# One program for the close of the first layer and the attention of the second: projections of the unscaled row, latent columns first, the output product in two halves by head kind

## The reference

```python
# end of the first block
x = x + g2 * moe_ffn(h, *moe_w).reshape(x.shape)
return rms_norm(x, final_norm_g)                  # x * rsqrt(mean(x*x) + 1e-6) * g

# second block
h = _rmsnorm(x, norm_mix_pre[l])
proj = h @ w_in[l]                                # 2208 columns
qa, ka, va, c_q, c_kv, k_r = jnp.split(proj, SPLIT_POINTS, axis=-1)   # 512, 512, 512, 384, 256, 32
ya = _dilated_attention(qa, ka, va)               # 8 heads of 64, distance bias and mask
yb = _mla(c_q, c_kv, k_r, q_lat_norm[l], w_uq[l], kv_lat_norm[l], w_ukv[l])
#    q = rmsnorm(c_q) @ w_uq, kv = rmsnorm(c_kv) @ w_ukv, 32 of 96 columns of q and k turned by the
#    token's angle, softmax(q k / sqrt(96)) v, 8 heads
y = jnp.concatenate([_rmsnorm(ya, out_norm_a[l]), _rmsnorm(yb, out_norm_b[l])], axis=-1)
y = y @ w_o[l]
x = x + _rmsnorm(y, norm_mix_post[l])
h = _rmsnorm(x, norm_ffn_pre[l])
u = _dwconv(h @ w_up[l], conv_w[l], conv_b[l])    # 5632 columns, three taps over the tokens
g, v = u[..., :D_FF], u[..., D_FF:]
y = (jax.nn.gelu(g, approximate=True) * v) @ w_down[l]
x = x + _rmsnorm(y, norm_ffn_post[l])
```

## Time and profile before

| | us |
|---|---|
| median of three runs (2211.8 to 2215.29) | 2213.43 |
| the profiled execution | 2209.3 |
| its span | 2207.5 |
| TensorE busy (88% of the span) | 1943.3 |
| VectorE busy | 622.6 |
| ScalarE busy | 435.8 |

### The profile page before, as it was taken

How to read it: one execution, slowest core, us unless ns; L and a number is a source line. 1 busy time by engine, 2 the same in 40 slices (tenths; PEclk the granted TensorE clock), 3 DMA queues, 4 the chain that set the end, 5 groups by cost and what they waited for, 6 DMA issues and landing times. The chain is left out here.

```text
span 2207.5 us, 24892 instructions
## 1 busy us (share of the span) xinstructions
PE 1943.3 (88%) x9274; PEld 1051.9 (48%) x9276; DVE 622.6 (28%) x1366; ACT 435.8 (20%) x849; POOL 67.1 (3%) x86
## 2 busy tenths in 40 slices
PE   5999796998989789989899999888889597879997
PEld 2446354987878443332333333333332245557774
DVE  2376355337420311111011111111111304333223
ACT  2221641345221111101111111111101114310111
POOL 1000400100000000000000000000000000000000
PEclk9999897899999899999999999999999899889998
DMA  9443336133454579999999999999999514033442
GB/s 343 152 172 116 143 99 153 66 104 114 163 184 165 228 298 416 418 418 419 418 419 417 418 418 417 417 417 418 417 419 418 204 58 165 0 116 143 155 158 86
DMA packets 150651, 566.73 MB, mean 257 GB/s; under 512 B 35872, under 2 KB 43808, under 8 KB 112736
## 3 DMA queue, kind: packets, MB, share of 16 engines
q1 hardware_dynamic: 150592, 565.91, 66.1%
HBM read 555.26 MB, written 10.62 MB: 256 GB/s over the span
## 5 line engine op out<-in xcount | busy, mean ns | idle before, releaser
L2005 PE MATMUL expert_gb<-expert_ring,hT 128*64 128x512 f32 x1024 | 270.4, 607 | 69.5 <-DMA expert_ring<-in_w_gu 68.1
L2005 PE MATMUL expert_lb<-expert_ring,hT 128*64 128x512 f32 x1024 | 262.8, 592 | 0.0
L1910 DVE TENSOR_SCALAR hT<-expert_gb 128x512 f32<-128x512 f32 x32 | 22.1, 692 | 717.1 <-PE expert_lb L2005 717.1
L2053 PE MATMUL expert_yb<-expert_ring,hT 128*64 128x512 f32 x512 | 222.7, 592 | 1.5 <-DMA expert_ring<-in_w_down 1.4
L2053 PE MATMUL expert_yb<-expert_ring,h2T 128*64 128x512 f32 x512 | 222.8, 592 | 0.0
L2005 PEld LDWEIGHTS expert_gb<-expert_ring,hT 128*64 128x64 f32 x1024 | 59.3, 135 | 250.2 <-DMA expert_ring<-in_w_gu 200.4
L2642 PE MATMUL ffn_pu<-ffn_hT,ffn_wu 128*128 128x256 f32 x704 | 156.5, 381 | 0.0
L2642 PEld LDWEIGHTS ffn_pu<-ffn_hT,ffn_wu 128*128 128x128 f32 x704 | 134.7, 191 | 27.4 <-issue 9.6
L445 PE MATMUL mix_in_pj<-hT,mix_in_pj_ring 128*128 128x512 f32 (+1 forms) x384 | 144.0, 533 | 4.0 <-DVE hT L566 4.0
L2005 PEld LDWEIGHTS expert_lb<-expert_ring,hT 128*64 128x64 f32 x1024 | 72.8, 137 | 147.0 <-issue 147.0
L2053 PEld LDWEIGHTS expert_yb<-expert_ring,hT 128*64 128x64 f32 x512 | 69.9, 137 | 143.2 <-issue 140.4
(11 more groups left out here) (474 smaller groups left out, 2314.1 us busy)
## 6 DMA issues: line engine op xcount, KB each, us to landing
expert_ring<-in_w_gu SPq DMA_DIRECT2D x256, 1024.0 KB, 19.7
expert_ring<-in_w_down SPq DMA_DIRECT2D x128, 1024.0 KB, 20.7
fill_w<-in_w_fill SPq DMA_DIRECT2D x48, 512.0 KB, 3.7
mix_in_wm<-in_w_mod SPq DMA_DIRECT2D x11, 2048.0 KB, 9.5
ffn_wu<-in_w_up_units SPq DMA_DIRECT2D x22, 1024.0 KB, 6.2
mix_in_pj_ring<-in_w_in_units SPq DMA_DIRECT2D x12, 1024.0 KB, 4.8
ffn_wd<-in_w_down SPq DMA_DIRECT2D x22, 512.0 KB, 3.4
attend_in_wi<-in_w_in SPq DMA_DIRECT2D x4, 2048.0 KB, 10.5
```

The source lines that it names most:

```text
L1910: v.tensor_scalar(glu, gb[j][:], LIMIT, None, ALU.min).then_inc(s_glu, 1)
L2005: m = pe.matmul(b[halves[h], :], xT[:, k, x], ring[:, z, c0 + 512 * h:c0 + 512 * h + 512], start=False, stop=(k == KT - 1))
L2053: m = pe.matmul(yb[h][halves[j], :], hidT[j][:, c, hh * SLOTS:(hh + 1) * SLOTS], ring[:, z, a * F + 512 * h:a * F + 512 * h + 512], start= ...
```

## The change

Blocks 1 to 4 become one block, `attend_stage`, of which the buffers lie in tensors of the first layer (the experts' ring holds w_in's blocks, `proj`, the bias, `qz`, `ka`, and later w_o, `qb`, `kb`). In it:

- TensorE transposes `S.x` as soon as a half of it is added. The product of the final gain and the second layer's first gain (`gg`) is multiplied in by the copies to `hT`, four column groups on ScalarE (`low`) and four on VectorE (`high`). The two roots are multiplied together (`rr`) and go into the copies of the products.
- w_in's blocks are taken in the order latent columns, rest of them, q, k, v; the latent columns are transposed unscaled, and their roots multiply the expansions in VectorE's copies. The expansions stand between the last groups of projections.
- the squares of the output of the first kind of heads, its transposes and its copies stand within the softmax steps (at 10, 12, 14 and 15); the output product is split into eight groups of four, first kind first, and `join` adds the two parts with their roots. The last row work is done by halves.
- in the feed-forward stage the first two units' up products are done by halves of tokens (`ups_half`), the root per half, and the matmuls that clear the sums come first.

```diff
-def close_first_stage(nc, A, C, S):
...
-                    link(v.tensor_tensor(S.acc[:, t, :], S.acc[:, t, :], S.g2, ALU.mult))
...
+    BLOCKS = [(3 * WA, 512), (3 * WA + 512, IN2 - 3 * WA - 512), (0, 512), (WA, 512), (2 * WA, 512)]
+    X = S.g
...
+        ring = Cut(S.ring[:].rearrange("p a n -> p (a n)"))
+        wi = ring(3, KT, 512)
+        proj = ring(2, IN2)
...
+                sp.dma_start(gcol[:], A.gains2_col).then_inc(s_gc, 16)
+                block_in(0)
+                sp.dma_start(gf, A.final_norm_g.to_broadcast([P, D])).then_inc(s_gf, 16)
+                block_in(1)
+                block_in(2)
+                sp.dma_start(wuq[:], A.w_uq.rearrange("(k p) n -> p k n", p=P)).then_inc(s_up, 16)
+                sp.dma_start(wukv, A.w_ukv.rearrange("(k p) n -> p k n", p=P)).then_inc(s_up, 16)
+                sp.dma_start(rope[:], A.rope).then_inc(s_up, 16)
+                sp.wait_ge(s_p, 2)
+                block_in(3)
+                sp.dma_start(bias, A.key_bias).then_inc(s_bias, 16)
+                sp.wait_ge(s_p, 4)
+                block_in(4)
+                sp.wait_ge(s_z, 2)
+                sp.dma_start(gpost, A.norm_mix_post.to_broadcast([P, D])).then_inc(s_wo, 16)
+                sp.wait_ge(s_p, 10)
+                sp.dma_start(wo, A.w_o.rearrange("(k p) n -> p k n", p=P)).then_inc(s_wo, 16)
+
...
+                    if v == 0:
+                        pe.wait_ge(s_ha, t + 1)
+                        pe.wait_ge(s_hd, t + 1)
+                    if g >= 4:
+                        pe.wait_ge(s_c, g - 3)
+                    for k in range(KT):
+                        m = pe.matmul(flat(4 + g % 4)[:, 0:n], hT[:, k, t * P:(t + 1) * P], wi[:, v % 3, k, 0:n],
+                                      start=(k == 0), stop=(k == KT - 1))
+                    m.then_inc(s_p, 1)
...
+                for t in range(2):
+                    pe.wait_ge(s_z, t + 1)
+                    for h in range(2):
+                        for k in range(4):
+                            m = pe.transpose(bank[2 * t + h][:, k, :], S.x[:, t, (4 * h + k) * P:(4 * h + k + 1) * P], C.ident)
+                        m.then_inc(s_t, 1)
+                for v in range(3):
                     for t in range(2):
...
+                        project(v, t)
+                pe.wait_ge(s_c, 4)
...
+                for t in range(2):
+                    project(3, t)
+                expand(0)
+                project(4, 0)
+                expand(1)
+                project(4, 1)
...
+                    if n in (10, 14):
+                        turn_out(0, n // 14, pY[n // 14])
+                pe.wait_ge(s_wo, 32)
+                multiply(0, 0, 0, bank[0])
+                multiply(0, 0, 1, bank[1])
+                turn_out(1, 0, pT[0])
+                turn_out(1, 1, pT[1])
+                multiply(0, 1, 0, bank[6])
+                multiply(0, 1, 1, bank[7])
+                multiply(1, 0, 0, bank[4])
+                multiply(1, 0, 1, bank[5])
+                pe.wait_ge(s_tc, 4)
+                multiply(1, 1, 0, bank[2])
+                multiply(1, 1, 1, bank[3])
+
...
+                def low(t):
+                    act.wait_ge(s_t, 2 * t + 1)
+                    for k in range(4):
+                        m = act.activation(hT[:, k, t * P:(t + 1) * P], bank[2 * t][:, k, :], ACT.Copy, scale=gg[:, k:k + 1])
+                    m.then_inc(s_ha, 1)
...
+                def copy(v, t):
+                    c, n = BLOCKS[v]
+                    g = 2 * v + t
+                    act.wait_ge(s_p, g + 1)
+                    act.activation(proj[:, t, c:c + n], flat(4 + g % 4)[:, 0:n], ACT.Copy,
+                                   scale=rr[:, t:t + 1]).then_inc(s_c, 1)
...
+                def square_out(a, t):
+                    act.wait_ge(s_y, 2 * a + t + 1)
+                    act.wait_ge(s_ys, 2 * a + t + 1)
+                    act.activation(junk[:, 0:WA], y[:, t, a, :], ACT.Square,
+                                   accum_out=stat[:, 6 + 2 * t + a:7 + 2 * t + a]).then_inc(s_ys, 1)
...
+                act.wait_ge(s_yr, 2)
+                act.activation(rstd[:, 6:10], stat[:, 6:10], ACT.Sqrt).then_inc(s_or, 1)
+                act.wait_ge(s_or, 1)
+                for t in range(2):
+                    for h in range(2):
+                        act.wait_ge(s_po, 2 * t + h + 1)
+                        act.activation(part[:, t, h, :], flat((0, 6)[t] + h), ACT.Copy,
+                                       scale=rstd[:, 6 + 2 * t:7 + 2 * t]).then_inc(s_f, 1)
+                for t in range(2):
+                    act.wait_ge(s_yo, 2 * t + 2)
+                    act.wait_ge(s_ys, 5 + t)
+                    act.activation(junk[:], yo[:, t, :], ACT.Square, accum_out=stat[:, 10 + t:11 + t]).then_inc(s_ys, 1)
+                    act.wait_ge(s_on, 2 * t + 2)
+                    act.activation(rstd[:, 10 + t:11 + t], stat[:, 10 + t:11 + t], ACT.Sqrt).then_inc(s_or, 1)
...
+                    v.tensor_tensor(S.acc[:, t, :], S.acc[:, t, :], S.g2, ALU.mult).then_inc(s_m, 1)
+                    v.wait_ge(s_m, t + 1)
+                    v.tensor_tensor(S.x[:, t, :], S.x[:, t, :], S.acc[:, t, :], ALU.add).then_inc(s_z, 1)
+                    if t == 0:
+                        v.wait_ge(s_gc, 16)
+                        v.tensor_tensor(gg[:], gcol[:, 0:KT], gcol[:, 2 * KT + 5:], ALU.mult).then_inc(s_gg, 1)
+                v.wait_ge(s_gg, 1)
+                high(0)
...
+                    v.scalar_tensor_tensor(X[:, t, :], S.x[:, t, :], rstd[:, t:t + 1], gf, ALU.mult, ALU.mult).then_inc(s_xd, 1)
+                v.wait_ge(s_sq, 4)
+                norm(v.tensor_scalar(stat[:, 10:12], stat[:, 10:12], 1.0 / D, EPS, ALU.mult, ALU.add))
+                norm(v.reciprocal(stat[:, 10:12], stat[:, 10:12]))
+                v.wait_ge(s_rt, 2)
+                v.tensor_tensor(rr[:], rstd[:, 0:2], rstd[:, 10:12], ALU.mult).then_inc(s_rr, 1)
...
+                        m = v.tensor_scalar(qc[:, t, 4 * g:4 * g + 4, :], src, rstd[:, 2 + t:3 + t], None, ALU.mult)
...
+                    if n in (7, 11, 15):
+                        take(n // 4 - 1)
+                    if n in (12, 15):
+                        gain(0, n // 15, pY[n // 15])
...
+                def join(t):
+                    for h in range(2):
+                        v.wait_ge(s_f, 2 * t + h + 1)
+                        v.wait_ge(s_po, 4 + 2 * t + h + 1)
+                        v.scalar_tensor_tensor(yo[:, t, 512 * h:512 * h + 512], flat((4, 2)[t] + h),
+                                               rstd[:, 7 + 2 * t:8 + 2 * t], part[:, t, h, :], ALU.mult, ALU.add).then_inc(s_yo, 1)
+                    v.wait_ge(s_ys, 6 + t)
+                    last(v.tensor_scalar(stat[:, 10 + t:11 + t], stat[:, 10 + t:11 + t], 1.0 / D, EPS, ALU.mult, ALU.add))
+                    last(v.reciprocal(stat[:, 10 + t:11 + t], stat[:, 10 + t:11 + t]))
+
+                def finish(t):
+                    v.wait_ge(s_or, 2 + t)
...
+                ups_half(0, 0)
+                turn(1)
+                ups_half(1, 0)
+                for z in range(2):
+                    ups_half(z, 1).then_inc(up[z], 1)
                 with pe.Fori(0, FT // 2 - 1) as i:
-                    ups(1, i * 16 + 16)
-                    downs(0, i + 1)
-                    ups(0, i * 16 + 32)
```

824 lines of the change are left out of this document (387 added, 437 removed).

## The result

The changed kernel takes 2173.49 us (median of 4 runs, 2170.69 to 2174.06), the kernel before 2212.61 us beside it (4 runs, 2210.33 to 2215.29). The ratio is 0.9822, 95% interval 0.9809 to 0.9835: 39.1 us less. Forecast were 42.0 us less and 2171.4 us. The profiled execution took 2173.72 us, its span is 2171.1.

A forecast was written before the change was run, and what follows sets the result against it. It took a chain of waits among TensorE, VectorE and ScalarE as the bound. Terms -13.1 - 14.3 + 0.9 - 13.4 - 2.1 + 0 gave -42.0 us; from 2213.4 that is 2171.4 us, range 2163 to 2183, chance 0.60.

The forecast's parts named there:

- front: First scaling to first projection: starts at 8.5 us instead of 21.6, waiting for the first weight block; -13.1 us.
- to the scores: First projection to first scores: 85.3 us instead of 99.65, from removed waits, program ends and half clock; -14.3 us.
- softmax loop: Sixteen softmax steps: inserted transposes cost TensorE time, squares and copies fit in other engines' slack; +0.9 us, bounds 0 and 5.1.
- product: Last value matmul to output product's end: starts without a pause, 28.7 us instead of 42.1; -13.4 us.
- tail: Output product's end to last add: half the rows finished earlier, 5.6 us left of 7.7; -2.1 us.
- border of the stages: Between the attention stage's last add and the feed-forward stage; the prediction's sum has no separate term for it.
- feed-forward head: First up products, split by token halves: earlier start and costs of halving cancel; 0 us, bounds -2.5 and +2.0.
- The new wait: Ahead of k's transposes, before the scores: TensorE stands 2.8 us until ScalarE has copied qz and ka.
- The first: Rival: loop inserts cost 5.1 us, product starts at half clock (1.7), new wait drops the clock (2.0); 2179.3 us, chance 0.22.
- The second: Rival: no half clock at start (1.0), wait hidden (2.8), loop free (0.9), feed-forward head -2.5; 2164.2 us, chance 0.12.
- The third: Rival: roots come late, so projections stand waiting for copies; each us is a us back, 15 lost gives 2186; chance 0.03.
- The fourth: Rival: chip grants only half clock through projections and product, +44.7 us net, 2258 us; chance 0.03.

The follow-up runs named there:

- roots_first: Changed kernel with the first projection also waiting for the joined scale (both roots); median 2178.2 us, ratio 0.985.
- expand_last: Changed kernel with both expansions of the latents behind the last projection again, latent columns still first; median 2174.0 us, ratio 0.9832.
- front_warm: Changed kernel with products of the unit matrix with itself filling TensorE's idle time in the front; median 2169.3 us, ratio 0.9815.
- before_again: The kernel before, unchanged, profiled a second time; 239.98 us from first scaling to first down product, against 239.78 in its first trace.
- product_waits: Changed kernel with the output product waiting for the output roots and the second kind's transposes ahead of it; median 2177.6 us, ratio 0.9851.
- gpost_late_whole: Changed kernel with the earlier feed-forward head (rows in one piece) and its wide gain row asked for behind the loop; median 2170.5 us, ratio 0.9818.
- joined_warm: Changed kernel with shared copies, first block in two transfers, whole feed-forward head, late wide row and unit-matrix products in the front; median 2163.7 us, ratio 0.9784.

## Why the prediction was right

The sum was 42.0, measured are 40.1 in the stretch and 39.1 in the median. By its own steps, against the first trace of the kernel before (the second would have moved product and feed-forward head by 1.6 and 0.8 us, in opposite directions):

| step | forecast | measured | |
|---|---|---|---|
| front | -13.1 | -13.3 | first projection 8.28 us in (8.5) |
| to the scores | -14.3 | -13.5 | projections 61.8, not 60.2 |
| softmax loop | +0.9 | +0.7 | |
| product | -13.4 | -13.7 | no idle, clock 1.00 |
| tail | -2.1 | -2.4 | last add 5.3 us after the product |
| border of the stages | 0 | +0.3 | 1.16 us before, 1.50 after |
| feed-forward head | 0 | +1.6 | inside its bounds, -2.5 to +2.0 |

**Front: right, and half of the reason shown.** The block landed 7.9 us after its issue (forecast 8.0), the scale was ready 14.3 us in (14.5), and roots_first gives back 6.2 us when the product waits for it. The reason for the other 7 us rests on the chain in the trace before, which is no longer there.

**To the scores: right but for the start.** The new wait is 2.80 us for 2.8 forecast, and expand_last shows the cover on VectorE. Wrong was "projections 59.2 + 1.0 for the cold start": TensorE was busy 61.8 us with them. front_warm, at full clock through all of them, has 60.0, so 0.8 us was missing from the 59.2 and the cold start cost 1.8, not 1.0. I had read from the earlier trace rows that transposes alone leave the clock at 1.00. In the new front transposes of the same kind stand in two groups of 8 with gaps, and the clock is 0.50 at 1748.5. TensorE: Matmul & The Clock Gate, Part 4, in the Trainium skill, has it that transposes don't bring the full clock. By that rule this term would be 2.0, closer than mine. The traces are divided on the rule: behind the same 16 transposes without a gap the clock was 1.00 once and 0.50 once (before_again). So my reading rested on one of two outcomes, and whether the gaps or the kind of instruction decide, no run here shows.

**Softmax and product: right.** The product is the largest single gain. product_waits shows that a part of it hangs on the start without a pause: waits of 2.5 us in all were followed by a clock near one half, 4.6 us together. The rest of the 13.7 (transposes and copies moved into the softmax steps) is read from the row of 12.9 us that is gone; no run puts it back. The three runs that bring a wait back return 6.2, 4.0 and 4.6 us, 14.8 of the 40. The table load stands at 1879.47, under the product, for 1.28 us. Of the drain that ScalarE: Activation LUTs, What ACT_TABLE_LOAD costs, in the Trainium skill, adds to a switch, product_waits shows none: there the load begins 0.01 us behind the square's sum and the root starts 0.34 us behind the load, waiting for VectorE.

**Feed-forward head: the step that failed.** It said that the earlier start and the costs of halving cancel. The first up product starts 9.1 us behind the stage's begin where before it was 10.4, a gain of 1.3 us and not the 2 that I had: `ffn_hT` was ready for 2.2, and the weights came 0.9 us later still. I had taken the gain row for the bound and not the weights behind it in the same queue. Against the 1.3 stand four costs, 2.9 us together. The 0.9 us of transposes and VectorE's 0.44 at the end were in the forecast. Two were not. The start is at half clock for longer: it costs 2.0 us (5.63 us until the second transposes, 3.6 at 113 ns a pass) where it cost 1.2 before (14.97 us for the 64 passes against 13.81 at full clock in gpost_late_whole), 0.8 more. And 128 half passes take 14.5 us at full clock where 64 whole ones take 13.8, 0.7 more; "no gain and little loss" was too kind. An earlier landing alone would not have mended it: in front_warm the up products start 1.1 us sooner than in the changed kernel, and the first down product only 0.6.

**Rivals.** The first was right in kind, in one of its three parts: the clock did fall at the new wait in 3 of 8 traces, for 1.5 to 2.6 us where I had 2.0, though not in the changed kernel's own. The second didn't happen, though joined_warm has the first of its four parts, the warm start, and about half of two more: a wait of 1.7 us instead of 2.8, and a head 1.3 us shorter than before instead of 2.5. The third didn't: the scale came with 3.0 us to spare for its first use by ScalarE, at 1757.54. The fourth didn't: behind the start the clock is 1.00 through the projections (1752.5 to 1829) and through softmax and product.

## What to carry to other kernels

When these programs were joined, the gain could be read from the trace before as the sum of the waits and chains at their borders: the four large terms came within 1 us. What a wait costs beyond its length is the clock behind it, and that part is not fixed: the pauses of 2 to 3 us here cost their length plus 0 to 2.6 us. Judge a small edit by landmarks of several traces, not by one, since the clock can hide a gain of 2 us or make up one; most edits here had one trace. Ask of each early start what it needs at the new time, down to the transfer behind the one that you looked at, and what clock it will start at: the split head began 1.3 us sooner, and what came behind cost it 2.9.

## What was not expected of the hardware

- The same wait of 2.80 us of TensorE, in the same place of the same program, was followed by a clock that stayed at 1.00 in five traces and fell to 0.50 in three. A wait of 1.93 us ahead of the product was followed by 0.57 for 2.1 us and 0.60 for 2.0.
- Sixteen transposes without a gap were followed by a clock of 1.00 in one trace of the kernel before (3.35 us) and by 0.50 in the other (3.67 us). Two groups of 8 with gaps of 0.5 and 1.3 us were followed by 0.50. With 16 products of the unit matrix in all ahead of and between them the clock was 1.00 at the first projection, both where it never fell (front_warm) and where it fell as they began and came back (joined_warm).
- A 2 MB transfer landed 7.87 us after its issue; asked for in two halves of 1 MB these landed after 5.35 and 7.60 us, and the first product started 1.5 us sooner. Nothing was lost by the second half.
- The part ahead of the stage varies by 5.6 us (1735.81 to 1741.45) between executions, while the 231 us behind the first down product vary by 0.1.
